# A two-layer DeltaNet and RWKV-7 backbone on one core: the norms' root on per-token sums, three tiles scaled ahead, weights split ahead, and two reordered DeltaNet stages

## The reference, cut to what matters

```python
x = x + 0.5*g1 * SwiGLU_1(mod1(RMSNorm(x)))
x = x + g2 * W_out [GatedDeltaNet heads | RWKV-7 heads](mod2(RMSNorm(x)))
x = x + 0.5*g3 * SwiGLU_2(mod3(RMSNorm(x)))
def rms_norm(x, gain):      # the gain is folded into the modulation's scale
    return x * rsqrt(mean(x*x, axis=-1) + 1e-6) * gain
```

## Time and profile before

| quantity | value |
|---|---|
| median of three runs | 5131.76 us |
| the profiled execution's own time | 5136.16 us |
| its span | 5134.5 us |
| PE busy | 4445.5 us, 87% |
| DVE busy | 2047.0 us, 40% |
| ACT busy | 1362.7 us, 27% |
| POOL busy | 536.2 us, 10% |

### The profile page before, as it was taken

How to read it: one execution, slowest core, us unless ns; L and a number is a source line. 1 busy time by engine, 2 the same in 40 slices (tenths; PEclk the granted TensorE clock), 3 DMA queues, 4 the chain that set the end, 5 groups by cost and what they waited for, 6 DMA issues and landing times. The chain is left out here.

```text
span 5134.5 us, 100832 instructions
## 1 busy us (share of the span) xinstructions
PE 4445.5 (87%) x43169; PEld 3918.9 (76%) x43169; DVE 2047.0 (40%) x2834; ACT 1362.7 (27%) x1954; POOL 536.2 (10%) x690
## 2 busy tenths in 40 slices
PE   6999969788866997899997999978887949996998
PEld 4998957687636996799896999865786729994786
DVE  3222244444466335422223222353443484436334
ACT  3211132222243222321113211232222242223322
POOL 1000000322023110000100000000321041100000
PEclk8999989799867998999999999988998959997999
DMA  5233221000200001233423222120001100002332
GB/s 182 82 106 113 75 86 41 1 1 0 73 7 2 4 4 63 74 115 106 148 82 98 66 57 66 45 62 21 1 0 33 47 0 4 4 5 93 98 96 68
DMA packets 341321, 286.28 MB, mean 56 GB/s; under 512 B 8766, under 2 KB 316452, under 8 KB 340004
## 3 DMA queue, kind: packets, MB, share of 16 engines
q1 hardware_dynamic: 323748, 218.92, 14.2%
q0 software_dynamic: 17280, 62.92, 3.5%
HBM read 270.27 MB, written 11.53 MB: 55 GB/s over the span
## 5 line engine op out<-in xcount | busy, mean ns | idle before, releaser
L626 PE MATMUL PS<-x_hi,w_hi 128*128 128x384 f32 (+1 forms) x2464 | 680.7, 345 | 78.2 <-DVE x_lo L531 73.3
L626 PE MATMUL PS<-x_lo,w_hi 128*128 128x384 f32 (+1 forms) x2464 | 676.6, 344 | 0.0
L626 PE MATMUL PS<-x_hi,w_lo 128*128 128x384 f32 (+1 forms) x2464 | 676.1, 343 | 0.0
L626 PEld LDWEIGHTS PS<-x_hi,w_hi 128*128 128x128 f32 x2464 | 448.8, 189 | 107.1 <-issue 41.6
L626 PEld LDWEIGHTS PS<-x_lo,w_hi 128*128 128x128 f32 x2464 | 450.7, 189 | 13.8
L626 PEld LDWEIGHTS PS<-x_hi,w_lo 128*128 128x128 f32 x2464 | 450.1, 189 | 14.0
L1758 PE MATMUL PS<-arena 64*64 64x64 f32 (+1 forms) x9216 | 385.3, 230 | 12.8 <-POOL arena L1741 5.5
L758 DVE TENSOR_TENSOR silu_buf<-silu_buf,PS 128x768 f32<-128x768 f32 (+1 forms) x88 | 78.1, 888 | 787.0 <-ACT silu_buf L691 787.0
L1758 PEld LDWEIGHTS PS<-arena 64*64 64x64 f32 x9216 | 355.4, 136 | 23.4 <-issue 16.2
L811 PE MATMUL PS<-p_hi,pw_hi 128*128 128x256 f32 (+1 forms) x1024 | 270.5, 347 | 112.2 <-DVE pw_lo L804 58.5
L669 PE MATMUL PS<-hidden_hi,w_hi 128*128 128x256 f32 (+1 forms) x1232 | 346.4, 351 | 19.4 <-DVE hidden_lo L763 19.4
(11 more groups left out here) (331 smaller groups left out, 7399.2 us busy)
## 6 DMA issues: line engine op xcount, KB each, us to landing
raw_w<-in_ffn_w_dram SPq DMA_DIRECT2D x240, 512.0 KB, 4.3
arena<-in_ada_w_dram POOLq DMA_DIRECT2D x120, 512.0 KB, 6.1
arena<-in_w_in_dram SPq DMA_DIRECT2D x64, 512.0 KB, 3.8
arena<-in_ada_w_dram SPq DMA_DIRECT2D x6, 2048.0 KB, 14.0
raw_w<-in_ffn_w_dram SPq DMA_DIRECT2D x32, 384.0 KB, 3.4
arena<-in_w_out_dram SPq DMA_DIRECT2D x16, 512.0 KB, 3.8
h_save<-arena SPq DMA_DIRECT2D x2, 3072.0 KB, 9.6
arena<-h_save SPq DMA_DIRECT2D x2, 3072.0 KB, 10.1
```

What stands on the lines that cost most here:

```text
L626: mm = pe.matmul(PS[:, 4 * b + 2 * g + s, 0:half], w[wo][:, k, g, :], x_split[xo][:, k, a + s * half:a + (s + 1) * half], start=(k == 0 an ...
```

## The change

1. The norm's root: PE sums per token with the sums as weights and a column of ones, into 128x6; ACT runs a small Sqrt (`warm`) ahead of its wait, then Sqrt on 128x6; DVE takes the reciprocal of 128x6 and multiplies the identity by it (`rstd_diag`, 128x768); PE multiplies ones by that diagonal into PSUM banks 6 and 7, and DVE scales from there. In all seven norms.
2. DVE scales three tiles ahead of the first low part, and ACT makes high(k) directly behind modulate(k).
3. In FFN norms the first weight block is split ahead of the root, and SP no longer waits for phases 1 and 10. In the projection's norm its two splits stay behind the root and, on DVE, behind the three scales.
4. h is saved tile by tile as the FFN's last part finishes each tile, no longer in one transfer at the start of phase 2.
5. The projection's split runs two products ahead, and its first pair is no longer written out.
6. The DeltaNet step: POOL does both directions' `DM` first, then `KTOK` and `DMT` of both, then the rest; DVE does both directions' `a`, x0 and X before both attn.

```diff
@@ -141,7 +142,7 @@
         sq_sum, sq_tile = region(15360, T), region(16128, 2, T)
-        rstd, rstd_ffn = region(41984, T), region(33280, T)
+        rstd_diag = region(16128, T // P, P)
         ADA_SLOTS = 4
@@ -493,47 +494,62 @@
+        RSTD = PS[:, 6:8, :].rearrange("p b c -> p (b c)")[:, CTX:]
...
         def pe_square_sum(pe, n, segs):
+            first = segs[0][0] // P
             pe.wait_ge(sq_summed, KT * n + KT - 1)
-            for s, (a, w) in enumerate(segs):
-                mm = pe.matmul(PS[:, s, 0:w], ones[:, :], sq_sum[:, a:a + w], start=True, stop=True)
+            for t in range(first, T // P):
+                mm = pe.matmul(PS[:, 0, t:t + 1], sq_sum[:, t * P:(t + 1) * P], ones[:, 0:1], start=True, stop=True)
             mm.then_inc(sq_summed, 1)
...
-        def act_root(act, n, segs, rstd=rstd):
+            pe.wait_ge(rstd_ready, 4 * n + 3)
+            for a, w in segs:
+                mm = pe.matmul(RSTD[:, a:a + w], ones[:, :], rstd_diag[:, a // P:(a + w) // P, :].rearrange("p t c -> p (t c)"),
+                               start=True, stop=True)
+            mm.then_inc(rstd_ready, 1)
...
+        def act_root(act, n, segs):
+            first = segs[0][0] // P
+            nc.scalar.activation(warm[:, :], eps[:, 0:1], ACT.Sqrt)
             act.wait_ge(sq_summed, KT * (n + 1))
-            for s, (a, w) in enumerate(segs):
-                ins = nc.scalar.activation(rstd[:, a:a + w], PS[:, s, 0:w], ACT.Sqrt, scale=1.0 / D_MODEL, bias=eps[:, 0:1])
-            ins.then_inc(rstd_ready, 1)
...
-        def dve_rstd(dve, n, segs, rstd=rstd):
-            dve.wait_ge(rstd_ready, 2 * n + 1)
+            nc.scalar.activation(tok_rms[:, first:], PS[:, 0, first:T // P], ACT.Sqrt, scale=1.0 / D_MODEL,
+                                 bias=eps[:, 0:1]).then_inc(rstd_ready, 1)
...
+        def dve_rstd(dve, n, segs):
+            first = segs[0][0] // P
+            dve.wait_ge(rstd_ready, 4 * n + 1)
+            nc.vector.reciprocal(tok_rms[:, first:], tok_rms[:, first:]).then_inc(rstd_ready, 1)
+            dve.wait_ge(rstd_ready, 4 * n + 2)
+            shape = [P, T // P - first, P]
+            nc.vector.tensor_tensor(rstd_diag[:, first:, :], bc(ident[:, :], 1, shape), bc(tok_rms[:, first:], 2, shape),
+                                    ALU.mult).then_inc(rstd_ready, 1)
+            dve.wait_ge(rstd_ready, 4 * n + 4)
...
+        x_high_ready, x_low_ready, h_saved = sem("x_high_ready"), sem("x_low_ready"), sem("h_saved")
...
+        def dve_norm_split(dve, n, segs, y, split, split_weights, h_saves=0):
...
             a = segs[0][0]
-            nc.vector.reciprocal(rstd[:, a:T], rstd[:, a:T]).then_inc(rstd_ready, 1)
-            dve.wait_ge(rstd_ready, 2 * n + 2)
...
-        x_high_ready, x_low_ready, h_saved = sem("x_high_ready"), sem("x_low_ready"), sem("h_saved")
...
-        def dve_norm_split(dve, n, segs, y, split, rstd, split_weights, h_saves=0):
...
-            a = segs[0][0]
             def scale(k):
-                nc.vector.tensor_tensor(y[:, k, a:T], h[:, k, a:T], rstd[:, a:T], ALU.mult).then_inc(normed, 1)
...
-            dve_rstd(dve, n, segs, rstd)
-            scale(0)
-            scale(1)
-            split_weights()
+                nc.vector.tensor_tensor(y[:, k, a:T], h[:, k, a:T], RSTD[:, a:T], ALU.mult).then_inc(normed, 1)
...
+            if not h_saves:
+                split_weights()
+            dve_rstd(dve, n, segs)
+            for k in range(3):
+                scale(k)
             if h_saves:
-                dve.wait_ge(h_saved, 16 * h_saves)
+                split_weights()
+                dve.wait_ge(h_saved, 16 * KT * h_saves)
             for k in range(KT):
...
                                         ALU.subtract).then_inc(x_low_ready, 1)
-                if k + 2 < KT:
-                    scale(k + 2)
...
-        def act_modulate(act, n, which, segs, y, split, rstd, split_weights):
+                if k + 3 < KT:
+                    scale(k + 3)
...
+        def act_modulate(act, n, which, segs, y, split, split_weights, weights_first):
@@ -541,8 +557,11 @@
-            act_root(act, n, segs, rstd)
-            split_weights()
+            if weights_first:
+                split_weights()
+            act_root(act, n, segs)
+            if not weights_first:
+                split_weights()
             for k in range(KT):
@@ -550,9 +569,7 @@
                 ins.then_inc(xn_ready, 1)
-                if k > 0:
-                    high(k - 1)
-            high(KT - 1)
+                high(k)
@@ -643,6 +660,7 @@
                     up(0, 0, True)
+                    pe.wait_ge(normed, KT * (norm + 1))
                     up(0, 1)
@@ -922,24 +940,19 @@
-            convolve(0, 0)
-            split(1, 0)
-            convolve(0, 1)
-            with act.Fori(1, 3 * NB // 2) as i:
+            with act.Fori(0, 3 * NB // 2) as i:
                 for b in range(2):
-                    if b == 0:
-                        split(i, 1)
-                    else:
-                        split(i + 1, 0)
+                    split(i + 1, b)
                     convolve(i, b)
...
             for z in range(NB):
-                split((3 * NB + z + 1) // 2, (z + 1) % 2)
                 for u in (2 * z, 2 * z + 1):
...
                 b = z % 2
+                if 3 * NB + z + 2 < DNB:
+                    split((3 * NB + z + 2) // 2, b)
                 act.wait_ge(proj_summed, 2 + layer * PT + 3 * NB + z + 1)
@@ -984,17 +997,11 @@
-            convolve(0, 0)
-            split(1, 0)
-            convolve(0, 1)
-            with dve.Fori(1, 3 * NB // 2) as i:
+            with dve.Fori(0, 3 * NB // 2) as i:
                 for b in range(2):
-                    if b == 0:
-                        split(i, 1)
-                    else:
-                        split(i + 1, 0)
+                    split(i + 1, b)
                     convolve(i, b)
-            for t in range(3 * NB + 1, DNB):
+            for t in range(3 * NB + 2, DNB):
                 split(t // 2, t % 2)
@@ -1154,11 +1161,15 @@
                     gp.tensor_tensor(DM[g], DM[g], row(bt), ALU.mult).then_inc(dm_weighted[g], 1)
+                for g in range(2):
                     pool.wait_ge(ktok_moved[g], it + 1)
...
                     gp.tensor_tensor(DMT[g], DMT[g], bc(upto_incl[:, :], 1, [P, DN_H, P]), ALU.mult).then_inc(dm_weighted[g], 1)
+                for g in range(2):
+                    u = slice(g * DN_H, (g + 1) * DN_H)
+                    row = lambda t: bc(t[:, bass.ds(first + i, 1), u].rearrange("p o u -> p (o u)"), 2, [P, DN_H, P])
                     pool.wait_ge(eb_ready[g], own + 1)
@@ -1399,7 +1411,10 @@
         def sp_save_h(sp, layer):
-            sp.dma_start(h_save, h[:, :, :].rearrange("p a b -> p (a b)")).then_inc(h_saved, 16)
+            done = 2 + 2 * layer * SUMS + (len(FF_PARTS) - 1) * KT
+            for k in range(KT):
+                sp.wait_ge(ffn_added, done + k + 1)
+                sp.dma_start(h_save[:, k * T:(k + 1) * T], h[:, k, :]).then_inc(h_saved, 16)
@@ -2208,7 +2223,6 @@
             pe.wait_ge(xn_ready, KT * (N_LAST + 1))
-            pe.wait_ge(rstd_ready, 2 * N_LAST + 2)
             for t in range(SEQ // P):
@@ -2243,10 +2257,9 @@
             for layer in range(DEPTH):
-                dma_after(sp, start_of(layer, 1))
                 sp_ffn(sp, 2 * layer, layer, 0)
+                sp_save_h(sp, layer)
                 dma_after(sp, start_of(layer, 2))
-                sp_save_h(sp, layer)
                 sp_proj_dn(sp, layer)
@@ -2258,7 +2271,6 @@
                 sp_wout(sp, layer)
-                dma_after(sp, start_of(layer, 10))
                 sp_ffn(sp, 2 * layer + 1, layer, 1)
@@ -2333,8 +2345,8 @@
                 end()
-                act_modulate(act, 3 * layer, 0, SEGS, xn_ffn, x_split, rstd_ffn,
-                             lambda: act_split(act, 2 * layer * BLOCKS, 0, 0))
+                act_modulate(act, 3 * layer, 0, SEGS, xn_ffn, x_split,
+                             lambda: act_split(act, 2 * layer * BLOCKS, 0, 0), True)
                 act_ffn(act, 2 * layer, 3 * layer + 1, SEGS)
```

More of the change, by code:

```diff
@@ L118, in build @@
         ab_raw = sb("ab_raw", [P, 6, 16])
+        tok_rms, warm = sb("tok_rms", [P, T // P]), sb("warm", [P, 1])
         band = sb("band", [P, 15])
@@ L972, in split_first @@
                     split(0, b)
[L974 removed]
+            dve_norm_split(dve, 3 * layer + 1, SEGS, xn_proj, p_split, split_first, layer + 1)
             def convolve(i, b):
@@ L1550, in act_feat @@
             ins.then_inc(kk_rooted, 1)
-            act.wait_ge(h_saved, 16 * (layer + 1))
+            act.wait_ge(h_saved, 16 * KT * (layer + 1))
             for u in range(2 * NB):
@@ L1629, in dve_feat @@
             dve.wait_ge(kk_step, n + 1 + 2 * NB)
-            dve.wait_ge(h_saved, 16 * (layer + 1))
+            dve.wait_ge(h_saved, 16 * KT * (layer + 1))
             for u in range(2 * NB):
```

(2 more changed lines are left out.)

11 lines of the change are left out of this document (5 added, 6 removed).

## The result

The changed kernel takes **5040.68 us** (median of 4 runs, 5037.1 to 5043.95), beside 5129.93 for the kernel before on the same chip: a ratio of 0.9824 with a 95% interval of 0.981 to 0.9838, so 89 us faster. The forecast was 5020 with a range of 4990 to 5048. The time lies in the range, 20.7 above the forecast: 112.0 us were forecast for the profiled execution, and 94.1 came (5136.16 less 5042.06).

What follows compares the result with a forecast made beforehand. PE was taken to bound the FFN blocks and to lose time at norms, projections and DeltaNet steps. Gains of 45.0 + 29.2 + 37.8 = 112.0 us from the profiled 5136.16 gave 5024.2, 5020 as median; range 4990 to 5048.

Steps and rivals of the forecast that it cites:

- Final norm: Last norm, without weights: long reciprocal, table load and root go, a diagonal and a spread come; 3.2 us gained.
- Its first product: Projection of layer 0: the first two products take 16.5 + 1.9 us, so the first is done 9.6 us better.
- The FFN norms: Norms 0, 2, 3, 5: second weight block 12.2, 9.9, 12.2, 7.5 us sooner; all norms with the final one 45.0.
- The projection's start: Projection's norm: weights no longer wait behind the save of h, so PE starts 8.2 us sooner in layer 0.
- The projection loop: Projection's loop: two table loads of 1.28 us a pair on the chain, 116.9 us for 112.7, 4.2 lost a layer.
- rival B: Projection loop: table loads hidden under ACT's wait for the convolution, 28 us come back, 4992; chance 0.14.
- The DeltaNet term: DeltaNet steps: DVE comes to the second direction's `a` 3.15 us sooner, in 12 steps 37.8 us gained.
- Rival D: Projection loop: PE's gaps drop the clock and it stays at 1.2 GHz, 68 us a layer lost, 5156; chance 0.02.
- Rival C: DeltaNet steps: PE's wait moves to attn or `QE`, so nothing of the 37.8 us comes, 5058; chance 0.15.

## Why the prediction was right, and where it was off

Times of layer 0 where not said otherwise, by the same two points in both traces.

| Step of the prediction | forecast gain | in the traces |
|---|---|---|
| Norm 0, sums to second block | 12.2 | 12.6 |
| Norm 2 | 9.9 | 10.6 |
| Norm 3 | 12.2 | 12.9 |
| Norm 5 | 7.5 | 7.8 |
| Final norm | 3.2 | 2.2 |
| Projection, start of PE | 8.2 | 8.3 |
| Its first product | 9.6 | 8.3 |
| Its loop | -4.2 | -4.1 |
| Behind the loop, z products | 0 | -1.8 |
| DeltaNet steps, of a layer | 18.9 | 13.4 |

- **The FFN norms** hold, to within 1 us each, and their sum of 45.0 came as 46. The pace of the tiles carries it, as argued: the run with the old order lost 57. The prices of the diagonal (0.96), the reciprocal (0.18 for 0.19), the root (0.25 for 0.3) and the scale out of PSUM (2.68 for three) were right, and the Trainium skill's rule on the shared port (SBUF — State Buffer, "Who interferes with whom") agrees with the 0.96: with no tensor operation of POOL beside it, two SBUF inputs cost what they do elsewhere. The token sums took 2.69 in norm 2 for a forecast of 2.7, and only 1.54 in norm 0, which hid behind ACT. What the text did not say plainly is that the new root gives some 6 us of this and the earlier weights next to nothing. The forecast had the second block wait for its split weights, and in norms 2, 3 and 5 it does: PE follows DVE's low part by 0.1 us, after waits of 0.22, 0.34 and 1.14. In norm 0 alone the weights are ready 0.4 us ahead of PE.
- **The projection's start** held in layer 0. In layer 1 PE was to start 10.3 us sooner, "by the same steps"; but these steps give some 8 there as well, and 8.4 came. The first product came 1.3 less early than forecast: ACT's split of 1.06 us, now two products ahead, stands between the first product and its copy (704.10 and 705.07). The forecast overlooked that instruction in the moved order.
- **The projection loop** held, table loads included, and rival B (4992) fell with the run that took the loads away. The forecast stopped at the loop's end. It gave PE's idle time of 2.9 us a pair as harmless, but behind the last product it comes in one piece: 8.17 us, then a granted clock of 0.78 over the next 10 us, 1.8 and 2.2 lost in the two layers. The two layers gave 20.9 us in place of 29.2.
- **The DeltaNet term** of 3.15 a step, 37.8, is the one that failed in size: 26.7 in the traces, 22.5 by the run that undid it. The order of the work was right to 0.4 us (the second `a` comes 3.54 sooner against the first). What failed is that the term took the saved wait for saved time. A part of the wait came back as one for X (6.5 to 17.2 us). The low clock of each step stayed 6.8 us long and moved from under the wait to under the heavy matmuls. The run with old order and filled gaps shows it: with the clock held, the term measures 41.8.
- **Rival D** had the right mechanism at the wrong place and size. The clock did not stay at 0.50 through the loop (the window reads 0.98). It cost some 2 us a layer behind it, and eleven in the DeltaNet steps, where the prediction did not look for it, though the earlier trace rows showed the price of an idle PE.
- **Rival C** (5058) fell: attn and `QE` are not waited for. PE's wait that grew is for X, 1.44 us a step.

The terms as measured give 46.1 + 20.9 + 26.7 = 93.7 of the 94.1 us. That is closer than it deserves: 1.5 us more came ahead of norm 0, some 3 scattered over phases that the change does not touch, and 4.0 were lost inside the FFNs (2.7 and 4.6 in layer 0, with 1.6 and 1.7 gained in layer 1). In two places of the 4.6, at 2242 and 2648 us, PE's products for the conditioning (L416) wait for the DMA of their weights and take 1.7 us longer each than before, when they ran there without a wait. Whether the change's earlier loads delay that DMA was not tried. The largest single loss is one stretch in the first FFN, where PE resumes after a wait of 3.03 us for a hidden tile (window after, and the window at the same place before):

```profile
604.50:611.30 6.80, 6.09 (x19) 5.22 (x20) 2.95 (x2) 1.33 (x1) 0.00 (x0) 0.50 0.26 81
```

```profile
618.00:624.80 6.80, 5.30 (x30) 4.70 (x31) 3.25 (x2) 2.12 (x2) 0.00 (x0) 1.00 0.15 44
```

Before, the clock there stayed at 1.00 behind the same wait; in the changed kernel's profile it fell to 0.50 for 6.8 us, which costs 2.7. In the profiles with the SiLU loaded first, the old loop, late weights and the old DeltaNet order it did not fall there, and all four had these 2.5 to 3 us back, though none of the edits touches this place. (The 22.5 us by which the old DeltaNet order was slower may therefore be 25.) So differences of 3 us between two kernels here say nothing of the edit. What decides it stays open.

## What to carry to other kernels

Read a saved wait on PE together with the granted clock around it: if a stretch of low clock lies under the wait, it will lie under work once the wait is gone, and cheap matmuls in the remaining gap can be worth more than the reordering. Order several engines so that one alone sets the pace before making any single instruction cheaper: here the tile order gave 57 us and a reciprocal 27 times shorter gave some 6. When a first iteration is folded into a loop of the device, look for table loads at the loop's head; one small activation of the loop's last kind ahead of it took 24 out of the two loops, 30 us.

## What of the hardware was not expected

- Extra transposes, 22 a DeltaNet step, made the kernel faster by 32 us: the granted clock over the steps of layer 0 went from 0.93 to 0.98. With 52 a step, 44 of them in one gap, the old order gained 13.
- A gap of 3.03 us ahead of the same matmul was followed by a clock of 1.00 in the kernel before and of 0.50 for 6.8 us in the changed one. The length of the gap alone does not tell.
- Three of POOL's products of a DeltaNet step changed places in price: `KTOK` from 1.07 to 1.50 us, `DMT` from 1.60 to 1.43, `QE` from 1.71 to 1.27 (means of 24 each, same shapes). The sum fell from 4.38 to 4.20 only. Which of DVE's instructions they meet differs with the order; that this is the cause was not tried.
